# Half-sized products for 55 groups instead of 42, with a plain group between the first two beats of a product run in three places

## The chip, the cores and the metric

The kernel runs on one core of a Trainium2 chip. The metric is the device time of one execution in microseconds, as the median of several runs. TensorE (PE) does the matmuls, VectorE (DVE) and ScalarE (ACT) prepare weights and evict results, GpSimd (POOL) does little here, and SyncE (SP) issues the DMA transfers.

## What is computed

The reference is a stack of transformer blocks on a sequence of 512 tokens with 1024 features. What matters here are its four gated feed-forward layers, in the order ffn1_in0, ffn2_in0, ffn1_in1, ffn2_in1 (an attention and retention mixer stands behind each ffn1, and nothing between ffn2 of layer 0 and ffn1 of layer 1):

```python
D_MODEL, D_FF, SEQ = 1024, 2816, 512
def swiglu(h, w_in, w_out):
    gu = h @ w_in
    a, b = gu[..., :D_FF], gu[..., D_FF:]
    return (jax.nn.silu(a) * b) @ w_out
...
x = x + 0.5 * swiglu(rmsnorm(x, norm_ffn1[l]), w_ffn1_in[l], w_ffn1_out[l])
...
x = x + 0.5 * swiglu(rmsnorm(x, norm_ffn2[l]), w_ffn2_in[l], w_ffn2_out[l])
```

## The kernel before

Everything on the chip is kept transposed: features lie along the 128 partitions and the 512 tokens along the free axis. A product in float32 accuracy is made of three matmuls per tile: weights and activations are split into a high part (fp32r) and a low part, and high times high, low times high and high times low are added up in a PSUM bank.

**Beats.** A planner (`Plan`) writes the whole program as a list of beats. A beat is what PE does with one buffer of 1024 weight columns; there are three such buffers (`w_hi`, `w_lo`, `SPLIT` = 3). Behind each beat the planner hangs a "tail": the work of the other engines, each engine's in the order in which the planner wrote it. The tail of beat i always begins with the split of the weights of beat i + 2: ACT writes `w_hi` (it has to wait until beat i - 1 is done, since it takes that beat's buffer), and DVE writes `w_lo` = raw - w_hi. Each engine works strictly through its own list, so a DVE operation waits for all that stands ahead of it.

**Groups.** A group is two output tiles (256 weight columns over all 1024 features). A plain group takes two beats of 24 matmuls each, 48 matmuls with 512 moving columns, into two banks. `take(2, True)` gives a plain group the free banks with the lowest numbers, of banks 0 to 3 as long as there are any. A product group does the same as seven products of half size in each dimension (Strassen's idea in another arrangement): 84 matmuls with 256 moving columns in four beats: first (two products), second (the forms "difference" and "second"), third (one product, form "third") and fourth (the form "fourth" among its two products). Below they are called A, B, C and D, with the number of the group. They are interleaved from one group to the next: A0 B0 A1 C0 B1 D0 A2 C1 B2 D1 and so on. DVE makes four sums of weight quarters for each group (`st_sum`, line 2813 before), four or five splits of weights (lines 2503 and 2510), three combinations of banks (line 2801), and then scales two tiles at once: `finish_silu` (line 2819, one operation) or, for a hidden group, `finish_hidden` (lines 2825 and 2830, two operations) and `hidden_low` (line 2839, one).

**Forms.** The products need sums of the activations. `make_forms` makes them once per layer: 8 ACT copies (line 2240), four DVE sums "difference", "second", "third" and "fourth" (lines 2849 to 2856), and a split of each on ACT (line 2245) and DVE (line 2860).

**Pieces.** A gated layer has two pieces, 12 and 10 groups, each followed by its part of the output product (`ffn*_out*`). Groups alternate: a silu group (two tiles of `a`), then the hidden group with the two tiles of `b` that belong to it. `by_products` says which groups of a piece are product groups: before, groups 4 to 9 of the first piece and 0 to 7 of the second in the last three layers, and none in ffn1_in0, 42 in all. A plain silu group is evicted by two DVE operations (line 2794); a plain hidden group by two pairs (lines 2655 and 2666) and, in later tails, two `hid_lo` operations (line 2521). In a layer with product groups those evictions are moved one tail back (`apart`).

The lines around a product beat, which set the order within a tail:

```python
        self.into = beat["tail"]
        self.flush()
        self.item("split_hi", i=i + AHEAD)
        self.item("split_lo", i=i + AHEAD)
        ...
        for fn in self.timed.pop(i, ()):
            fn()
        self.run_later()
```

`flush` writes what the beat before has left (copies and combinations), `timed` holds the work of `make_forms`, and `run_later` the evictions that were put off.

Of the kernel before, what the change touches and what calls it, by code (L numbers as in the profile page):

```python
# [7 lines left out]
P = 128  # L8
S = 512
# [38 lines left out]
PLAIN_FIRST = {"ffn1_in0": (12, 10), "ffn2_in0": (4, 0), "ffn1_in1": (4, 0), "ffn2_in1": (4, 0), "mlp_in": (6, 5, 5)}  # L48
# [39 lines left out]
def by_products(name, piece, n_groups):  # L88

    return [PLAIN_FIRST[name][piece] <= i < n_groups - 2 for i in range(n_groups)]  # L90

# [96 lines left out]
class Plan:  # L188
# [59 lines left out]
    def gemm(self, name, n_k, groups, src, evict, first_k=0, n=S, rows=None, tok=None, fresh=True):  # L248


        for tiles in groups:
# [4 lines left out]
            for k0, nk in unit_blocks(n_k, len(tiles)):  # L256
# [7 lines left out]
                beat["load"] = self.load(i, name, at, cols)  # L264
# [136 lines left out]
    def seven_products(self, name, out, finish):  # L401
# [36 lines left out]
        def after_second(units=self.units()):  # L438
            self.copy_out(st, "u2", units, sums[0], 1, LEFT)
        self.waiting.append(after_second)  # L440

        def third():
            self.product_beat([piece(0, second, 0, "t3")], [product("third", 0, sums, False, "u2")])

            def after_third(units=self.units()):
                self.copy_out(st, "u3", units, sums[0], 1, RIGHT)
                self.combine(st, "c22", units, apart[0], 1, RIGHT, "u3", "subtract")
            self.waiting.append(after_third)

        def fourth():  # L450
            first["last"] = second["last"] = self.units()
            self.product_beat([piece(0, first, QUARTER, "t4"), piece(QUARTER, second, QUARTER, None)],
                              [product("right_last", 0, sums, False, "u3"), product("fourth", QUARTER, apart, False, "c22")])

            def after_fourth(units=self.units()):
                self.copy_out(st, "c21", units, sums[0], 0, RIGHT)
                self.bank_over[sums] = ("st_copied", st["c21"])
                self.combine(st, "c12", units, apart[0], 1, LEFT, "u2", "subtract")
                self.bank_over[apart] = ("st_combined", st["c12"])
# [9 lines left out]
    def make_forms(self):  # L469


        start = self.stage_start = self.units()
# [7 lines left out]
        def form(name):  # L480
            it = self.item("form", name=name, values=self.count["form_value"], out=self.add("form"),
# [989 lines left out]
def build(nc, x_in, vec_in, ident_in, tri_in, decay_in, rope_in, sel_in, mem_in, onehot_in, band_in, table_in,  # L1471
# [4 lines left out]
    with ctx:  # L1476
# [140 lines left out]
        def product(it, o):  # L1617

            return bank[it["pair"][o]]
# [1614 lines left out]
```

## Time and profile before

| | |
|---|---|
| median of 3 runs | 3102.11 us (3101.87 to 3102.22) |
| the profiled execution's own time | 3101.85 us |
| its span | 3100.1 us |
| granted TensorE clock, mean | 0.998 |
| PE busy | 3076.7 us, 99% |
| DVE busy | 1782.4 us, 57% |
| ACT busy | 1231.6 us, 40% |
| DMA engines' mean share | 29.2%, 300.78 MB |

A share is an average over the whole span. A matmul's record is longer than the distance between the starts of two matmuls, since they are pipelined: rates are read from a stretch of time and the number of matmuls in it, and idle time of PE only shows where it is longer than that overlap.

### The profile page before, as it was taken

The numbers are of one execution on the slowest core, as the hardware profiler recorded it, in microseconds if no ns is written. First come the engines' busy times: TensorE is split into PE (matmuls) and PEld (weight loads), VectorE is DVE, ScalarE is ACT, GpSimd is POOL, SyncE is SP. The second block draws the span as 40 slices with busy tenths as digits, with TensorE's granted clock in tenths as the row PEclk, the third lists the DMA queues.
The fourth block names the chain that finished last, engine by engine and source line by source line (L and its number), as shares of the span: only waits on it lengthen the run. The fifth ranks groups of instructions, "written<-read, shape, count | busy, mean of one in ns | idle before, by whom it ended". The sixth has DMA issues, their size and how long they took to land.

```text
span 3100.1 us, 40065 instructions
## 1 busy us (share of the span) xinstructions
PE 3076.7 (99%) x15846; PEld 2575.9 (83%) x15846; DVE 1782.4 (57%) x2887; ACT 1231.6 (40%) x1871; POOL 252.9 (8%) x223
## 2 busy tenths in 40 slices
PE   9999999999999999999999999999999999999998
PEld 7888887778889889898877788999888877888887
DVE  6434436555856758495455557758656555563543
ACT  5323335434534445253344335434556433332222
POOL 0000103102000010000031020000300000110001
PEclk9999999999999999999999999999999999999999
DMA  5222322222423232323222232223322233323232
GB/s 157 96 95 93 132 92 72 75 75 95 143 96 109 86 119 86 106 96 130 93 71 75 69 102 102 96 96 109 117 99 87 85 99 99 100 97 100 87 100 78
DMA packets 95930, 303.35 MB, mean 98 GB/s; under 512 B 11184, under 2 KB 21808, under 8 KB 95036
## 3 DMA queue, kind: packets, MB, share of 16 engines
q1 hardware_dynamic: 95744, 300.78, 29.2%
q8 instruction: 127, 2.08, 0.3%
q14 instruction: 59, 0.48, 0.1%
HBM read 298.59 MB, written 5.29 MB: 98 GB/s over the span
## 4 chain that ended last, share of the span: by engine, by line
PE 97%; DVE 1%; issue 0%; DMA 0%; ACT 0%; SPq 0%; POOLq 0%; POOL 0%; DVEq 0%; ACTq 0%
PE bank L2018 77%; PE bank L2047 7%; PE score_ps L2047 4%; PE out_ps L2047 1%; PE score_ps L2018 1%; PE score_ps L1845 1%; PE out_ps L1878 1%; PE turn_ps L1856 1%; PE out_ps L1897 1%; PE score_ps L1887 1%; PE score_ps L1919 1%; PE out_ps L2018 1%; PE score_ps L1969 0%; PE turn_ps L1865 0%; PE turn_ps L1794 0%
## 5 line engine op out<-in xcount | busy, mean ns | idle before, releaser
L2510 DVE TENSOR_TENSOR w_lo<-raw,w_hi 128x1024 fp32r<-128x1024 f32 (+1 forms) x469 | 570.4, 1217 | 861.7 <-ACT w_hi L2080 860.5
L2080 ACT ACTIVATE w_hi<-raw 128x1024 fp32r<-128x1024 f32 (+1 forms) x469 | 479.5, 1024 | 834.1 <-PE bank L2018 763.5
L2018 PE MATMUL bank<-in_hi,w_hi 128*128 128x512 f32 x1960 | 787.8, 402 | 2.0 <-DVE in_lo L2516 1.1
L2018 PE MATMUL bank<-in_hi,w_lo 128*128 128x512 f32 x1960 | 764.9, 390 | 0.0
L2018 PE MATMUL bank<-in_lo,w_hi 128*128 128x512 f32 x1960 | 764.5, 390 | 0.0
L2018 PEld LDWEIGHTS bank<-in_hi,w_hi 128*128 128x128 f32 x1960 | 368.2, 188 | 96.9 <-issue 20.5
L2018 PEld LDWEIGHTS bank<-in_hi,w_lo 128*128 128x128 f32 x1960 | 367.9, 188 | 79.4
L2018 PEld LDWEIGHTS bank<-in_lo,w_hi 128*128 128x128 f32 x1960 | 368.6, 188 | 74.0 <-issue 2.4
L2018 PE MATMUL bank<-hid_hi,w_hi 128*128 128x512 f32 x960 | 374.0, 390 | 0.0
L2018 PE MATMUL bank<-hid_lo,w_hi 128*128 128x512 f32 x960 | 373.5, 389 | 0.0
L2018 PE MATMUL bank<-hid_hi,w_lo 128*128 128x512 f32 x960 | 373.5, 389 | 0.0
L2018 PEld LDWEIGHTS bank<-hid_hi,w_hi 128*128 128x128 f32 x960 | 180.2, 188 | 37.9 <-DVE hid_lo L2839 0.8
L2018 PEld LDWEIGHTS bank<-hid_hi,w_lo 128*128 128x128 f32 x960 | 180.2, 188 | 37.5
L2018 PEld LDWEIGHTS bank<-hid_lo,w_hi 128*128 128x128 f32 x960 | 180.2, 188 | 37.3
L2415 POOL TENSOR_TENSOR ssum<-ssum,tmp 128x512 f32<-128x512 f32 x55 | 77.7, 1412 | 1509.1 <-ACT tmp L2101 1506.2
L2503 DVE TENSOR_TENSOR w_lo<-raw_more,w_hi 128x512 fp32r<-128x512 f32 (+1 forms) x135 | 105.1, 791 | 53.8 <-ACT w_hi L2089 53.5
L2089 ACT ACTIVATE w_hi<-raw_more 128x512 fp32r<-128x512 f32 (+1 forms) x135 | 93.9, 711 | 89.1 <-PE bank L2018 88.1
L2047 PE MATMUL bank<-form_hi_t,w_hi 128*128 128x256 f32 x384 | 109.5, 285 | 5.2 <-DVE w_lo L2503 5.2
L2655 DVE TENSOR_TENSOR tmp<-bank,rstd_b 128x512 f32<-128x512 f32 x153 | 101.2, 683 | 18.1 <-PE bank L2018 15.5
L2047 PE MATMUL bank<-form_lo_t,w_hi 128*128 128x256 f32 x384 | 108.6, 283 | 0.0
L2047 PE MATMUL bank<-form_hi_t,w_lo 128*128 128x256 f32 x384 | 108.6, 283 | 0.0
L2220 ACT ACTIVATE hid_hi<-tmp 128x512 fp32r<-128x512 f32 x78 | 49.0, 632 | 111.8 <-DVE tmp L2666 61.0
(428 smaller groups left out, 4911.9 us busy)
## 6 DMA issues: line engine op xcount, KB each, us to landing
raw<-w_ffn_in SPq DMA_DIRECT2D x121, 512.0 KB, 3.3
raw<-w_mix SPq DMA_DIRECT2D x90, 512.0 KB, 3.3
raw<-w_ffn_out SPq DMA_DIRECT2D x80, 512.0 KB, 3.3
raw<-w_mixb SPq DMA_DIRECT2D x58, 512.0 KB, 3.3
raw_more<-w_ffn_in SPq DMA_DIRECT2D x54, 512.0 KB, 4.6
raw<-w_mlp_in SPq DMA_DIRECT2D x32, 512.0 KB, 3.3
raw<-w_mlp_out SPq DMA_DIRECT2D x28, 512.0 KB, 3.3
raw<-w_w_out SPq DMA_DIRECT2D x16, 512.0 KB, 3.2
```

The costliest lines, as they stand in the source:

```text
L1845: mm = pe.matmul(score[k][:, 0:keys], DST["fq"][hp][64 * k:64 * k + 64, i * P:(i + 1) * P], DST["fk"][hp][64 * k:64 * k + 64, 0:keys], sta ...
L1856: mm = pe.transpose(turn_ps[:, b * P:(b + 1) * P], p[:, b * P:(b + 1) * P], ident[:])
L1878: mm = pe.matmul(out_ps[64 * k:64 * k + 64, i * P:(i + 1) * P], fv[:, b, h * FDH:(h + 1) * FDH], pt[:, b * P:(b + 1) * P], start=b == 0, s ...
L2018: mm = pe.matmul(ps, lhs, rhs, start=first and step == 0, stop=last and step == 2, skip_group_check=True)
L2047: mm = pe.matmul(ps, y, x, start=part["start"] and k == 0 and step == 0, stop=k == TT - 1 and step == 2, skip_group_check=True)
L2080: act.activation(w_hi[:, i % SPLIT, cut], raw_at(ld)[:, cut], ACT.Copy).then_inc(S_["hi_split"], 1)
L2089: hi = act.activation(w_hi[:, i % SPLIT, to], source(part), ACT.Copy)
L2220: act.activation(SRC["hid"][0][part["h"]], tmp[part["t"].b], ACT.Copy).then_inc(S_["hid_hi"], 1)
L2415: pool.tensor_tensor(dst, dst, tmp[s["place"].b][:, 0:n], ALU.add).then_inc(S_["ssum_add"], 1)
L2503: lo = dve.tensor_tensor(w_lo[:, i % SPLIT, to], source(part), w_hi[:, i % SPLIT, to].bitcast(F32), ALU.subtract)
L2510: dve.tensor_tensor(w_lo[:, i % SPLIT, cut], raw_at(ld)[:, cut], w_hi[:, i % SPLIT, cut].bitcast(F32), ALU.subtract).then_inc(S_["lo_split ...
L2655: dve.tensor_tensor(tmp[t.b], product(it, o), RSTD["rstd"], ALU.mult).then_inc(S_["dve_evict"], 1)
```

## The change

Product groups become 55. ffn1_in0 gets groups 8 and 9 of its first piece and 0 to 7 of its second; its forms are made 9 beats later than the layer's start (`FORM_DELAY`), and their first sum waits until six small transfers (`bias_moved`) have left the memory that it overlays. In the first pieces of the other three layers, groups 3 and 5 to 10 are product groups: group 3, a hidden group, is the first product group, and group 4, a plain silu group, stands with its first beat between A and B of group 3 and with its second beat between B and C. Only the last group, a hidden one, stays plain at the end, its two beats between the last groups' C and D. The second pieces of these three layers keep their order. The form "fourth" is made before "third". The plain groups of such a layer may load their weights into the four extra buffers (`raw_more`) too. The values and raw forms lie elsewhere in memory, in two halves.

```diff
-PLAIN_FIRST = {"ffn1_in0": (12, 10), "ffn2_in0": (4, 0), "ffn1_in1": (4, 0), "ffn2_in1": (4, 0), "mlp_in": (6, 5, 5)}
+PLAIN_FIRST = {"ffn1_in0": (8, 0), "ffn2_in0": (3, 0), "ffn1_in1": (3, 0), "ffn2_in1": (3, 0), "mlp_in": (6, 5, 5)}
+FORM_DELAY = {"ffn1_in0": (9, 16 * 6)}
...
 def by_products(name, piece, n_groups):
 
-    return [PLAIN_FIRST[name][piece] <= i < n_groups - 2 for i in range(n_groups)]
+    first = PLAIN_FIRST[name][piece]
+    if piece or name == "ffn1_in0":
+        return [first <= i < n_groups - 2 for i in range(n_groups)]
+    return [first <= i < n_groups - 1 and i != first + 1 for i in range(n_groups)]
...
-        if self.left:
-            self.left.popleft()()
-        self.weight_sums(st, self.beats[-1], "t3", "t4")
-        apart = self.bank_over.take(1)
-        self.product_beat([piece(0, first, 0, "t1"), piece(QUARTER, "t2", 0, "t2")],
-                          [product("difference", 0, apart, True), product("second", QUARTER, sums, False, "m1")])
...
+        def others():
+            self.weight_sums(st, self.beats[-1], "t3", "t4")
+            apart = st["apart"] = self.bank_over.take(1)
+            self.product_beat([piece(0, first, 0, "t1"), piece(QUARTER, "t2", 0, "t2")],
+                              [product("difference", 0, apart, True), product("second", QUARTER, sums, False, "m1")])
...
+        if plain_next and not self.left:
+            self.left.extend([others, third, fourth])
+            return
+        if self.left:
+            self.left.popleft()()
+        others()
         if self.left:
             self.left.popleft()()
         self.left.extend([third, fourth])
...
-                                  lambda: form("second"), lambda: split("difference"), lambda: split("second"),
-                                  lambda: form("third"), lambda: split("third"), lambda: form("fourth"),
+                                  lambda: form("second"), lambda: split("difference"), lambda: form("fourth"),
+                                  lambda: split("second"), lambda: form("third"), lambda: split("third"),
                                   lambda: split("fourth"))):
-            self.after(n + 1, work)
+            self.after(delay + n + 1, work)
```

How the instructions move at the places of which the prediction speaks:

PE at the start of the product run in the first piece of ffn2_in0, before: the first matmul of each part, with the semaphores it waits for (`dve_evict` counts DVE's evictions).

```order
L2018 MATMUL bank_0<-in_hi,w_hi 128x512 [waits lo_split]
L2047 MATMUL bank_2<-in_hi,w_hi 128x256 [waits dve_evict,lo_split]
L2047 MATMUL bank_3<-in_hi,w_hi 128x256 [waits dve_evict]
L2047 MATMUL score_ps<-form_hi_t,w_hi 128x256 [waits form_lo,ret_weighted,lo_split]
L2047 MATMUL bank_2<-form_hi_t,w_hi 128x256 [waits form_lo,st_copied]
```

The same place now.

```order
L2030 MATMUL bank_1<-in_hi,w_hi 128x512 [waits lo_split]
L2059 MATMUL bank_2<-in_hi,w_hi 128x256 [waits dve_evict,lo_split]
L2059 MATMUL bank_0<-in_hi,w_hi 128x256 [waits dve_evict]
L2030 MATMUL bank_1<-in_hi,w_hi 128x512 [waits lo_split,dve_evict]
L2059 MATMUL score_ps<-form_hi_t,w_hi 128x256 [waits form_lo,ret_weighted,lo_split]
L2059 MATMUL bank_2<-form_hi_t,w_hi 128x256 [waits form_lo,st_copied]
```

Between A (banks 2 and 0) and B (`score_ps`) there is now a plain beat into bank 1 (and 3), and the plain group ahead of A had the same pair of banks.

DVE in the tails of the beat A and of the plain beat behind it, first piece of ffn2_in0, now. The first two rows split B's weights; the two `silu_t` rows evict the plain group that stood ahead of A.

```order
L2515 TENSOR_TENSOR w_lo<-raw_more,w_hi 128x512 [waits hi_split]
L2515 TENSOR_TENSOR w_lo<-second_sum,w_hi 128x512
L2874 TENSOR_TENSOR form_lo_t<-form_t,form_hi_t 128x1024 [waits form_hi]
L2533 TENSOR_TENSOR hid_lo<-tmp,hid_hi 128x512 [waits hid_hi] x2
L2806 TENSOR_TENSOR silu_t<-bank_1,rstd_b 128x512 [waits gated,unit_used,rstd]
L2806 TENSOR_TENSOR silu_t<-bank_3,rstd_b 128x512 [waits gated]
L2522 TENSOR_TENSOR w_lo<-raw,w_hi 128x1024 [waits hi_split]
L2825 TENSOR_TENSOR raw<-raw 128x512
```

Before, that eviction stood in the tail two beats ahead of A; A itself took its banks, and a plain beat of another group lay between.

DVE from the tail of A to the split for D at the only new product run in a first piece, ffn1_in0, now (group 8; the `w_lo` rows split the weights of C, then of the next group's B, then of D).

```order
L2867 TENSOR_TENSOR form_t<-form_first 128x1024 [waits form_value,bias_moved]
L2667 TENSOR_TENSOR tmp<-bank_2,rstd_b 128x512 [waits hid_lo,unit_used,rstd]
...
L2813 TENSOR_TENSOR silu_t<-bank_1,silu_t 128x256 [waits st_copied,unit_used]
L2515 TENSOR_TENSOR w_lo<-raw_more,w_hi 128x512 [waits hi_split]
L2874 TENSOR_TENSOR form_lo_t<-form_t,form_hi_t 128x1024 [waits form_hi]
L2515 TENSOR_TENSOR w_lo<-raw_more,w_hi 128x512 [waits hi_split]
L2515 TENSOR_TENSOR w_lo<-second_sum,w_hi 128x512
L2874 TENSOR_TENSOR form_lo_t<-form_t,form_hi_t 128x1024 [waits form_hi]
L2533 TENSOR_TENSOR hid_lo<-tmp,hid_hi 128x512 [waits hid_hi] x2
L2813 TENSOR_TENSOR tmp<-out_ps,tmp 128x256 [waits st_copied,unit_used]
L2515 TENSOR_TENSOR w_lo<-raw,w_hi 128x512 [waits hi_split]
```

The same stretch in ffn2_in0 before: one `form_lo_t` row (that of "fourth") instead of two (those of "third" and "fourth").

```order
L2801 TENSOR_TENSOR silu_t<-bank_3,silu_t 128x256 [waits st_copied,unit_used]
L2503 TENSOR_TENSOR w_lo<-raw_more,w_hi 128x512 [waits hi_split]
L2860 TENSOR_TENSOR form_lo_t<-form_t,form_hi_t 128x1024 [waits form_hi]
L2503 TENSOR_TENSOR w_lo<-raw_more,w_hi 128x512 [waits hi_split]
L2503 TENSOR_TENSOR w_lo<-second_sum,w_hi 128x512
L2521 TENSOR_TENSOR hid_lo<-tmp,hid_hi 128x512 [waits hid_hi] x2
L2801 TENSOR_TENSOR tmp<-out_ps,tmp 128x256 [waits st_copied,unit_used]
L2503 TENSOR_TENSOR w_lo<-raw_more,w_hi 128x512 [waits hi_split]
```

There the sum "third" and its split were done before B; now they stand behind A in ffn1_in0, and B to D follow without a plain beat between.

## Rows read from the trace of the kernel before

**Rows 1.** The page: busy time, share of the span and instructions of each engine.

```profile
PE 3076.7 (99%) x15846; PEld 2575.9 (83%) x15846; DVE 1782.4 (57%) x2887; ACT 1231.6 (40%) x1871; POOL 252.9 (8%) x223
```

**Rows 2.** The page: the chain that ended last, by engine.

```profile
PE 97%; DVE 1%; issue 0%; DMA 0%; ACT 0%; SPq 0%; POOLq 0%; POOL 0%; DVEq 0%; ACTq 0%
```

**Rows 3.** Waits of PE: us in total, times, longest.

```profile
PE bank L2047 <- DVE w_lo L2503: 6.1, 8, 1.1
```

**Rows 4.** Windows: a stretch of plain groups, a second piece's product run.

```profile
208.27:317.07 108.80, 108.80 (x481) 90.12 (x480) 47.23 (x56) 31.99 (x38) 0.00 (x0) 1.00 0.29 94
...
1311.75:1388.18 76.43, 76.43 (x637) 76.38 (x636) 71.38 (x108) 42.56 (x79) 0.00 (x0) 1.00 0.23 79
```

**Rows 5.** Windows: the product runs of the three first pieces.

```profile
809.75:868.92 59.17, 57.01 (x469) 56.38 (x468) 55.95 (x84) 32.95 (x60) 0.00 (x0) 1.00 0.19 65
1161.95:1220.33 58.38, 56.64 (x470) 56.27 (x469) 55.80 (x84) 32.71 (x60) 0.00 (x0) 1.00 0.19 64
1908.16:1967.33 59.17, 57.00 (x469) 56.37 (x468) 55.95 (x84) 32.94 (x60) 0.00 (x0) 1.00 0.19 63
```

**Rows 6.** Timeline of PE: C0, B1 and D0 in the first piece of ffn2_in0.

```profile
819.63 0.36 PE L2047 MATMUL bank<-form_hi_t,w_hi 128*128 128x256 f32 x1 [1.09 <-DVE w_lo L2503]
...
821.95 0.39 PE L2047 MATMUL bank<-form_hi_t,w_hi 128*128 128x256 f32 x1 [0.65 <-DVE w_lo L2503]
...
825.51 0.39 PE L2047 MATMUL bank<-in_hi,w_hi 128*128 128x256 f32 x1 [0.43 <-DVE w_lo L2503]
```

**Rows 7.** Timeline of DVE at the same place.

```profile
818.84 0.68 DVE L2503 TENSOR_TENSOR w_lo<-raw_more,w_hi 128x512 fp32r<-128x512 f32 x1
819.44 1.22 DVE L2860 TENSOR_TENSOR form_lo_t<-form_t,form_hi_t 128x1024 fp32r<-128x1024 f32 x1
820.60 0.69 DVE L2503 TENSOR_TENSOR w_lo<-raw_more,w_hi 128x512 fp32r<-128x512 f32 x1
...
824.16 1.29 DVE L2503 TENSOR_TENSOR w_lo<-raw_more,w_hi 128x512 fp32r<-128x512 f32 x2 [0.64 <-ACT w_hi L2089]
```

**Rows 8.** Timeline of PE: the first matmul of the plain beat ahead of A0.

```profile
804.31 0.39 PE L2018 MATMUL bank<-in_hi,w_hi 128*128 128x512 f32 x1
```

**Rows 9.** Timeline of ACT: split in two halves, a hidden tile, a silu pair.

```profile
804.51 0.63 ACT L2089 ACTIVATE w_hi<-raw_more 128x512 fp32r<-128x512 f32 x1 [4.38 <-PE bank L2018]
805.05 0.61 ACT L2089 ACTIVATE w_hi<-second_sum 128x512 fp32r<-128x512 f32 x1
...
818.63 0.63 ACT L2220 ACTIVATE hid_hi<-tmp 128x512 fp32r<-128x512 f32 x1 [0.70 <-DVE tmp L2666]
...
832.98 1.05 ACT L2231 ACTIVATE silu_t<-silu_t 128x1024 f32<-128x1024 f32 x1
```

**Rows 10.** Timeline of DVE in the two tails ahead of A0.

```profile
803.90 1.29 DVE L2521 TENSOR_TENSOR hid_lo<-tmp,hid_hi 128x512 fp32r<-128x512 f32 x2
805.10 1.28 DVE L2794 TENSOR_TENSOR silu_t<-bank,rstd_b 128x512 f32<-128x512 f32 x2
806.30 0.68 DVE L2503 TENSOR_TENSOR w_lo<-raw_more,w_hi 128x512 fp32r<-128x512 f32 x1
...
807.51 1.21 DVE L2860 TENSOR_TENSOR form_lo_t<-form_t,form_hi_t 128x1024 fp32r<-128x1024 f32 x1
```

**Rows 11.** Timeline of DVE in a product run, ffn2_in0's second piece.

```profile
987.92 0.69 DVE L2503 TENSOR_TENSOR w_lo<-raw,w_hi 128x512 fp32r<-128x512 f32 x1 [0.85 <-ACT w_hi L2089]
...
1000.46 1.22 DVE L2819 TENSOR_TENSOR silu_t<-silu_t,rstd_b 128x1024 f32<-128x1024 f32 x1
...
1009.38 1.22 DVE L2825 TENSOR_TENSOR tmp<-tmp,rstd_b 128x1024 f32<-128x1024 f32 x1
...
1017.44 1.22 DVE L2839 TENSOR_TENSOR hid_lo<-tmp,hid_hi 128x1024 fp32r<-128x1024 f32 x1
...
1020.71 1.22 DVE L2819 TENSOR_TENSOR silu_t<-silu_t,rstd_b 128x1024 f32<-128x1024 f32 x1
```

**Rows 12.** Timeline of DVE: the eviction of a plain hidden pair, first of four.

```profile
815.86 0.68 DVE L2655 TENSOR_TENSOR tmp<-bank,rstd_b 128x512 f32<-128x512 f32 x1
```

More of the change, by code:

```diff
@@ L246, in flush, with gemm @@
             fn()
-    def gemm(self, name, n_k, groups, src, evict, first_k=0, n=S, rows=None, tok=None, fresh=True):
+    def gemm(self, name, n_k, groups, src, evict, first_k=0, n=S, rows=None, tok=None, fresh=True, more=0):
         for tiles in groups:
@@ L263, in gemm @@
                             bank_over=[], others_over=[], half=None, new_k={}, products=None)
-                beat["load"] = self.load(i, name, at, cols)
+                beat["load"] = self.load(i, name, at, cols, more)
                 beat["load"]["last"] = i
@@ L399, in weight_sums, with seven_products @@
             beat["split_end"] += 1
-    def seven_products(self, name, out, finish):
+    def seven_products(self, name, out, finish, plain_next):
         if not self.many_banks:
@@ L452, in fourth @@
             self.product_beat([piece(0, first, QUARTER, "t4"), piece(QUARTER, second, QUARTER, None)],
-                              [product("right_last", 0, sums, False, "u3"), product("fourth", QUARTER, apart, False, "c22")])
+                              [product("right_last", 0, sums, False, "u3"), product("fourth", QUARTER, st["apart"], False, "c22")])
             def after_fourth(units=self.units()):
@@ L467, in form_at, with make_forms @@
         return self.forms.get(form, 0)
-    def make_forms(self):
-        start = self.stage_start = self.units()
+    def make_forms(self, delay, bias):
+        start = self.stage_start = max(self.units(), 1)
         self.forms = {}
@@ L480, in form @@
         def form(name):
-            it = self.item("form", name=name, values=self.count["form_value"], out=self.add("form"),
+            it = self.item("form", name=name, bias=bias, values=self.count["form_value"], out=self.add("form"),
                            source=self.vals.get("form_" + {"second": "difference", "fourth": "second"}.get(name, "")))
@@ L714, in feed_forward @@
                 made = True
-                self.make_forms()
+                self.make_forms(*FORM_DELAY.get(w_in, (0, 0)))
             for i, (tiles, by_seven) in enumerate(zip(groups, seven)):
@@ L724, in evict @@
                             evict_in(outs, units, pair)
-                    self.gemm(w_in, DT, [tiles], self.inp, evict, fresh=tiles is groups[0])
+                    self.gemm(w_in, DT, [tiles], self.inp, evict, fresh=tiles is groups[0],
+                              more=self.stage_start if made else 0)
                     continue
@@ L734, in feed_forward @@
                     awaiting.add(j)
-                    self.seven_products(w_in, out, lambda st, j=j: finish_silu(st, j))
+                    self.seven_products(w_in, out, lambda st, j=j: finish_silu(st, j),
+                                        not (seven + [False])[i + 1])
                 else:
-                    self.seven_products(w_in, out, lambda st, j=j: finish_hidden(st, j))
+                    self.seven_products(w_in, out, lambda st, j=j: finish_hidden(st, j), not (seven + [False])[i + 1])
             assert not self.left
@@ L1626, in product_rows @@
             return bank[it["pair"][o // 2]][:, (o % 2) * 256:(o % 2) * 256 + 256]
-        form_hi, form_lo, form_raw, form_values = m["form_hi_t"], m["form_lo_t"], m["form_t"], m["form_values"]
+        form_hi, form_lo, form_raw = m["form_hi_t"], m["form_lo_t"], m["form_t"]
+        form_values = tiles(m["form_first"]) + tiles(m["form_last"])
         def raw_at(ld):
@@ L2239, in work @@
                     act.wait_ge(S_["unit_used"], it["units"])
-                    act.activation(form_values[:, it["j"], :], xT[it["j"]], ACT.Copy,
+                    act.activation(form_values[it["j"]], xT[it["j"]], ACT.Copy,
                                    scale=gain(dict(it["part"], j=it["j"]))).then_inc(S_["form_value"], 1)
@@ L2843, in work @@
                     dst, before = form_raw[:, f_:f_ + TT, :], form_raw[:, f_ - TT:f_, :]
-                    first, last = form_values[:, 0:TT, :], form_values[:, TT:DT, :]
+                    first, last = m["form_first"], m["form_last"]
+                    if it["bias"]:
+                        dve.wait_ge(S_["bias_moved"], it["bias"])
                     dve.wait_ge(S_["form_value"], it["values"])
```

16 lines of the change are left out of this document (8 added, 8 removed).

## The prediction

> **What bounds the kernel now.** I read the page first: PE is busy for 3076.7 us of a span of 3100.1 [rows 1], and the chain that ended last is 97% PE [rows 2]. So the time is the number of matmuls times their distance, plus the few places where PE waits. The waits of PE come next: in the product stretches it waits for one thing only, DVE's `w_lo`, 8 times and 6.1 us in all [rows 3]. What a matmul costs must be read from windows, since the records overlap. A stretch of 10 plain groups, 480 matmuls, takes 108.80 us, which is 0.2267 us each; a second piece's run of 636 half-width matmuls takes 76.43 us, 0.1202 each [rows 4]. In the same window DVE is busy for 71.38 of 76.43 us: in a product stretch two engines are near their limit, and DVE's 57% on the page hides that. The timeline of DVE shows how near. Its last wait there ends at 987.92; from the `finish_silu` at 1000.46 to the next at 1020.71, two groups later, it takes 20.25 us [rows 11], while PE needs 2 x 84 x 0.1202 = 20.19. DVE can be ahead only by the little that the three weight buffers allow. So I ask of each moved piece of work when DVE does it, not how much it is.
>
> **Fewer matmul columns.** 13 groups change from plain to products: 10 in ffn1_in0, one in each of the three other layers. A plain group is 48 x 0.2267 = 10.88 us, a product group 84 x 0.1202 = 10.10 [rows 4]. That is 0.78 us saved for each, **-10.2 us**. The seven products have 7/8 of the columns, but a matmul of half the width costs 53% of a full one, not 50%, and so the saving is 7%, not 12.5%.
>
> A rule of the Trainium skill would make this larger: "TensorE: Matmul & The Clock Gate", section "Back-to-back issue gap", gives N/2.4 + 2.5 ns for the isolated gap between matmuls at the full clock. By it a product group would be 84 x 109.2 = 9.17 us, a plain one 48 x 215.8 = 10.36, the saving 15.4 us and my sum some 5 us lower. The trace does not agree at either width (120.2 and 226.7 ns), so its rows are used.
>
> **What the old starts cost.** The product runs of the three first pieces are 468 matmuls each, 56.25 us at 0.1202, and take 59.17, 58.38 and 59.17 us [rows 5]. So 2.9 + 2.1 + 2.9 = 7.9 us are lost there. The timeline of PE shows where: C0, B1 and D0 of the first run start late, each behind a `w_lo` [rows 6], and DVE's timeline says why: in these tails it still makes and splits a form and evicts the last plain groups (a `form_lo` lies ahead of B1's weights, 820.60) [rows 7]. In the new order plain beats of 24 x 0.2267 = 5.44 us stand between A and B and between B and C. In each DVE has one weight split of 1.2 us and the forms, so it is done with "third" and "fourth" before C and D come. I take all of it as gone: **-7.9 us** (0 to -7.9).
>
> **A new wait for a bank, three times.** The plain beat behind A takes the very pair of banks that the plain group ahead of A has filled. Their eviction stands in A's own tail, behind the split of B's weights, the split of the form "second" and two `hid_lo`. The trace before has this chain in pieces. ACT starts the two half splits 0.20 us after PE's beat begins and ends them at +1.35 (804.31 to 805.66) [rows 8, 9]. DVE then has two half `w_lo`, 1.21 us from start to start of the next (806.30 to 807.51); the form's split, 1.16 (819.44 to 820.60); two `hid_lo`, 1.20 (803.90 to 805.10); and two `silu_t` evictions, 1.28 [rows 7, 10]. With 0.1 for the hand-over to DVE and 0.1 to PE this is 1.35 + 0.1 + 1.21 + 1.16 + 1.20 + 1.28 + 0.1 = 6.4 us after A's start. A lasts 24 x 0.1202 = 2.88. PE waits for 3.5 us, in each of the three layers: **+10.5 us**. Below: an eviction that had nothing of the form and the `hid_lo` ahead of it would still be 1.2 us late (6.4 - 1.16 - 1.20 - 2.88), so 1.2 each; above 4.5, if ACT or a late `hid_hi` costs another 1.0. I keep 3.5, since every link is a strict order on one engine. Behind the waiting plain beat stand only matmuls; ACT's and DVE's next splits depend on beats already done, so DVE catches up in this time, and the start that follows is the freer.
>
> **Two hidden groups in a row, three times.** The run used to alternate silu and hidden groups. Now group 3 (hidden) is followed by group 5 (hidden). DVE's finish of a hidden group is three operations of 1.22 us, that of a silu group one; taking these 4 x 1.22 = 4.9 from 20.25, a group's common part is 7.7 us [rows 11]. So a hidden group costs DVE 11.3 us against PE's 10.1, a debt of 1.2; a silu group 8.9, which pays it back. Two hidden ones in a row make a debt of 2.4, and what DVE can be ahead is about one debt (before, single ones were carried with no wait on the page). I take 1.2 us in each layer, **+3.6** (0 to 2.4 each).
>
> **The start in ffn1_in0.** Here A, B, A, C, B, D follow each other as in the old starts, so the old loss comes back, 2.9 us [rows 5]. And it is worse by one form: "third" is now summed behind A and split just ahead of C, "fourth" is split behind it, where before only "fourth" stood there. C needs "third" itself; the split ends where `form_lo` ends now, one operation of 1.1 us later than C0's start [rows 6, 7], and D0's weights come later by the same operation. I take 2.9 + 1.1 = **+4.0 us** (2.1 to 5.1). The 8 values and the 4 forms themselves (some 9 us on either engine) lie under plain beats in which DVE is busy for less than half of the time (47.23 of 108.80) [rows 4]; without that cover they would cost 9 us. The wait for `bias_moved` stands some 12 beats in, long after these transfers.
>
> **The end of the first pieces.** Only one plain group is left behind the last silu group's products. Its hidden pair needs that silu: D ends, then come a combination and `finish_silu` in the first output beat, in the second the silu on ACT, which stands behind a weight split that cannot begin before +5.6 (done at 7.7, with 1.05 each), then four evictions of 0.68 on DVE and the last `hid_hi` and `hid_lo` of 0.63 and 0.65 [rows 9, 10, 12]: 7.8 + 2.7 + 0.7 + 0.7 = 11.9. PE wants the last tile at the fourth step of the third output beat, 10.88 + 9 x 0.2267 = 12.9. I cost it at **0**, hidden by two output beats with 1.0 to spare; with one more us of delay it starts to show (0 to 1.0 each).
>
> No transfer is added (a product group loads the same megabyte), and none of SP's or POOL's queue is moved past another; the loads in these pieces are issued sooner.
>
> **Sum.** -10.2 - 7.9 + 10.5 + 3.6 + 4.0 = 0.0. On the profiled execution's own time, 3101.85 us, that is **3101.9 us**; the median of the runs shown is 3102.1, 0.3 above it.
>
> **Rivals.** (1) The new bank wait is not there, because DVE reaches that eviction early. Then the sum is lower by 10.5: 3091. For it speaks only that DVE is idle when A starts; against it the order of the tail, which the plan fixes. (2) DVE never gets ahead in the new runs. Then each of the three hidden groups among the five that finish inside a run costs its full debt of 1.25, 3.75 per layer instead of 1.2: +7.7, 3109.5, which is slower than before. It decides from about 3.3 us per layer. The windows speak for it (55.95 busy of 59.17) [rows 5]; against it that the old runs lost their 2.9 at the start and no more after it, and that the new start leaves DVE two plain beats of rest. (3) The end of the piece shows, by up to 1.0 us in each layer, 3105: a small addition, inside the range. (4) Less is lost in all three disputed places (bank wait 3.0, hidden pair 0, ffn1_in0 2.1): -1.5 - 3.6 - 1.9, 3095.
>
> **How the numbers follow.** A difference of 0.2%, 6.2 us, is about what a measurement here can tell from none; faster is below 3095.9, slower above 3108.3. Forecast, the sum with its small shifts: 0.66. Rival 1: 0.11. Rival 2: 0.11. Rival 4 down to and below 3095.9: 0.08. The old loss partly staying at the new starts, by about 2 us per layer, 3108: 0.04, of which 0.03 slower. Faster 0.19, same 0.67, slower 0.14. The range leaves out rival 1 and the upper half of rival 2: 3095 to 3109.5.
>
> **What would show it.** In the trace after: PE's waits for DVE's `silu_t` eviction, three, of about 3.3 us each (the overlap of records hides 0.16), at the first plain beat behind the first product beat in ffn2_in0, ffn1_in1 and ffn2_in1. No wait for `w_lo` at C0, B1 and D0 there, but one or two of about 1 us some four groups' beats later, at the beats behind the second hidden group's finish. In ffn1_in0's first piece waits of C0 and D0 with 4 us lost in all. The run of its second piece at 0.120 us a matmul. The forecast fails most easily by the bank wait, which is the largest term and was never seen before, and by DVE's debt, which hangs on tenths of a microsecond.

## The result and the profile after

The changed kernel takes 3106.86 us (median of 20 runs, 3103.47 to 3109.16), the kernel before 3102.11 us on the same chips (20 runs, 3101.66 to 3102.57). The ratio is 1.0014, with a 95% interval of 1.0008 to 1.002: slower by 0.14%, some 4.7 us. The forecast was 3101.9 us, no change. The value lies in its range, yet it was off by 5.0 us, and "no change" did not come true: the kernel is slower by more than the measurement is uncertain. The prediction took 0.2%, 6.2 us, for about what can be told from no difference; with 20 runs of each kernel the interval reaches 0.06% to either side. Note also the spread: 5.7 us after, 0.9 us before. The profiled execution took 3108.83 us, near the slow end of that spread.

The page of the changed kernel, busy times and chain; compare [rows 1, 2].

```profile
span 3107.0 us, 41348 instructions
...
PE 3074.3 (99%) x16314; PEld 2595.0 (84%) x16314; DVE 1858.9 (60%) x3009; ACT 1275.8 (41%) x1974; POOL 252.9 (8%) x223
...
PE 96%; DVE 2%; issue 1%; ACT 1%; DMA 0%; SPq 0%; POOL 0%; POOLq 0%; ACTq 0%; DVEq 0%
```

PE is busy for 2.4 us less, and the span is 6.9 us longer: the chain's share of DVE went from 1% to 2%. Where PE waits for DVE now (us in total, times, longest), against [rows 3]:

```profile
PE bank L2030 <- DVE silu_t L2806: 10.7, 4, 3.2
...
PE bank L2059 <- DVE form_lo_t L2874: 2.3, 1, 2.3
...
PE bank L2059 <- DVE tmp L2813: 1.7, 3, 0.6
```

The `w_lo` waits of the old starts are gone from the product runs. In their place stand the three bank waits that were forecast, with a fourth wait for `silu_t` of 1.0 that was not, one for the split of a form, and three for a combination.

The timeline of PE at the first bank wait: the last matmul of A, and the plain beat that takes the banks of the group ahead of A.

```profile
800.39 0.28 PE L2059 MATMUL bank<-in_hi,w_lo 128*128 128x256 f32 x1
803.91 0.79 PE L2030 MATMUL bank<-in_hi,w_hi 128*128 128x512 f32 x1 [3.24 <-DVE silu_t L2806]
804.50 0.63 PE L2030 MATMUL bank<-in_lo,w_hi 128*128 128x512 f32 x1
...
809.62 0.60 PE L2030 MATMUL bank<-in_lo,w_hi 128*128 128x512 f32 x1
810.05 0.41 PE L2030 MATMUL bank<-in_hi,w_lo 128*128 128x512 f32 x1
810.29 0.39 PE L2030 MATMUL bank<-in_hi,w_hi 128*128 128x512 f32 x1
```

From start to start the gap is 803.91 - 800.39 = 3.52 us, 3.40 more than the 0.12 of a matmul (3.5 was forecast). But look at the durations behind it: 0.63 instead of 0.39, and from 804.50 to 809.62 the distance from start to start is twelve times the same, 5.12 us in all, 0.4267 each instead of 0.2267. PE had run at the full clock up to this wait and comes out of it at half of it. The windows of the start (columns: from and to, length, busy time and number of instructions of PE, weight loads, DVE, ACT and POOL, granted clock, DMA share, GB/s) show the clock, first behind each wait in the three layers, then over each whole start, the 96 matmuls from A to the last plain beat:

```profile
803.91:810.05 6.14, 6.14 (x15) 4.79 (x16) 3.75 (x5) 0.61 (x2) 0.00 (x0) 0.50 0.28 88
1159.81:1165.95 6.14, 6.14 (x29) 5.13 (x30) 3.75 (x5) 0.94 (x3) 0.00 (x0) 1.00 0.24 88
1907.69:1913.83 6.14, 6.14 (x20) 4.91 (x21) 3.75 (x5) 0.61 (x2) 0.00 (x0) 0.72 0.25 85
...
797.63:820.70 23.07, 19.83 (x97) 16.89 (x96) 14.29 (x18) 8.63 (x12) 0.00 (x0) 0.85 0.22 59
1153.54:1173.77 20.23, 16.99 (x98) 14.82 (x96) 14.29 (x18) 8.64 (x12) 0.00 (x0) 1.00 0.11 40
1901.42:1923.21 21.79, 18.55 (x98) 15.96 (x96) 14.30 (x18) 8.52 (x12) 0.00 (x0) 0.92 0.11 38
```

0.50 is the lower of TensorE's two levels (1.2 GHz), 1.00 the upper (2.4 GHz), and 0.72 a stretch of both. The three waits have the same length and the same cause, 3.24 us in the records; one is followed by 14 slow matmuls, one by 8, one by none. That is why the three starts take 23.07, 20.23 and 21.79 us. The second, at the full clock, shows what the wait alone costs: 3.55 us more than the same start without a wait (16.68, in e1 below), 0.15 more than its 3.40, since the first distances behind it are a little longer too (0.34 and 0.24 us before they settle at 0.2267). The Trainium skill, "TensorE: Matmul & The Clock Gate", section "Wait — 56ns, not 53.3ns?", gives exactly N ÷ 1.2 GHz from start to start for a cold array, 426.7 ns at 512 columns; the trace agrees, with 0.4267.

The timeline of DVE at the same wait has the chain link by link:

```profile
799.02 0.69 DVE L2515 TENSOR_TENSOR w_lo<-raw_more,w_hi 128x512 fp32r<-128x512 f32 x1 [2.23 <-ACT w_hi L2101]
799.63 0.68 DVE L2515 TENSOR_TENSOR w_lo<-second_sum,w_hi 128x512 fp32r<-128x512 f32 x1
800.23 1.22 DVE L2874 TENSOR_TENSOR form_lo_t<-form_t,form_hi_t 128x1024 fp32r<-128x1024 f32 x1
801.37 1.29 DVE L2533 TENSOR_TENSOR hid_lo<-tmp,hid_hi 128x512 fp32r<-128x512 f32 x2
802.57 1.28 DVE L2806 TENSOR_TENSOR silu_t<-bank,rstd_b 128x512 f32<-128x512 f32 x2
```

A starts at 797.63, `silu_t` ends at 803.85, PE goes on at 803.91: 6.28 us, against 6.4 forecast.

Windows of the product runs (A, C, B, D and so on, without a plain beat between) in the three first pieces, then the first piece's and the second piece's run of ffn1_in0:

```profile
820.70:882.28 61.58, 61.03 (x505) 60.69 (x504) 58.90 (x88) 35.69 (x66) 0.00 (x0) 1.00 0.26 89
1173.77:1235.33 61.56, 61.01 (x505) 60.67 (x504) 58.88 (x88) 35.76 (x66) 0.00 (x0) 1.00 0.26 87
1923.21:1984.78 61.57, 61.02 (x506) 60.68 (x504) 58.89 (x88) 35.68 (x66) 0.00 (x0) 1.00 0.27 86
101.84:121.66 19.82, 17.55 (x134) 17.37 (x133) 17.90 (x26) 10.09 (x17) 0.00 (x0) 0.91 0.08 27
213.08:289.52 76.44, 76.44 (x637) 76.39 (x636) 71.40 (x108) 42.59 (x79) 0.00 (x0) 1.00 0.25 93
```

504 matmuls at 0.1202 are 60.58 us; 1.0 us is lost in each, where 1.2 was forecast. In ffn1_in0's first run 19.82 - 132 x 0.1202 = 3.95 us are lost (4.0 forecast), and there too the clock is not 1.00. Its second run goes at 0.1202.

Where the first of these runs loses its 1.0 us, on PE and on DVE:

```profile
840.12 0.39 PE L2059 MATMUL bank<-form_hi_t,w_hi 128*128 128x256 f32 x1 [0.55 <-DVE tmp L2813]
```

```profile
838.52 1.22 DVE L2851 TENSOR_TENSOR hid_lo<-tmp,hid_hi 128x1024 fp32r<-128x1024 f32 x1
839.65 0.42 DVE L2813 TENSOR_TENSOR tmp<-bank,tmp 128x256 f32<-128x256 f32 x1
...
844.71 1.22 DVE L2837 TENSOR_TENSOR tmp<-tmp,rstd_b 128x1024 f32<-128x1024 f32 x1
```

PE is at the second half of D of group 5, the second hidden group, and waits for the combination at 839.65, which stands behind the `hid_lo` of group 3. From start to start 0.71 us are lost here, the rest in steps of 0.1 behind it. The finish of group 5 begins at 844.71 only.

The books of the profiled execution against that of before, all from starts of matmuls: the stretch from the first plain beat of each piece to the first matmul of its second piece's run, ffn2_in0, 177.92 us before and 181.64 after, +3.72; ffn1_in1 +1.65; ffn2_in1 +2.43; ffn1_in0 with both pieces 344.12 and 341.79, -2.33. That is +5.5 of 6.9. Another 1.1 us lies in the first 28 us of the program, ahead of every change (27.35 before, 28.43 after); this place differs from one execution to the next (26.80 to 27.56 in the traces of the experiments, 27.05 and 27.39 in e5 and e6, which are alike up to there) and is chance.

### The profile page after: what moved, and what is told of

The parts are those of the page before. It is cut to its first block, busy times and chain, and to the rows that moved or that the text cites. A ratio compares the mean times of both kernels' runs of the same rounds, so it can differ in the third digit from the quotient of the medians.

```text
span 3107.0 us, 41348 instructions
## 1 busy us (share of the span) xinstructions
PE 3074.3 (99%) x16314; PEld 2595.0 (84%) x16314; DVE 1858.9 (60%) x3009; ACT 1275.8 (41%) x1974; POOL 252.9 (8%) x223
## 4 chain that ended last, share of the span: by engine, by line
PE 96%; DVE 2%; issue 1%; ACT 1%; DMA 0%; SPq 0%; POOL 0%; POOLq 0%; ACTq 0%; DVEq 0%
PE bank L2030 73%; PE bank L2059 9%; PE score_ps L2059 5%; PE out_ps L2059 2%; PE score_ps L2030 1%; PE score_ps L1857 1%; PE out_ps L1890 1%; PE turn_ps L1868 1%; PE out_ps L1909 1%; PE score_ps L1899 1%; PE score_ps L1931 1%; PE out_ps L2030 0%; PE score_ps L1981 0%; PE turn_ps L1877 0%; ACT w_hi L2101 0%
## 5 line engine op out<-in xcount | busy, mean ns | idle before, releaser
L2522 DVE TENSOR_TENSOR w_lo<-raw,w_hi 128x1024 fp32r<-128x1024 f32 (+2 forms) x414 | 503.3, 1217 | 727.1 <-ACT w_hi L2092 725.8
L2030 PE MATMUL bank<-in_hi,w_hi 128*128 128x512 f32 x1760 | 712.6, 405 | 13.6 <-DVE silu_t L2806 10.7
L2092 ACT ACTIVATE w_hi<-raw 128x1024 fp32r<-128x1024 f32 (+2 forms) x414 | 421.7, 1020 | 731.3 <-PE bank L2030 658.2
L2030 PE MATMUL bank<-in_lo,w_hi 128*128 128x512 f32 x1760 | 688.7, 391 | 0.0
L2030 PE MATMUL bank<-in_hi,w_lo 128*128 128x512 f32 x1760 | 688.6, 391 | 0.0
L2030 PEld LDWEIGHTS bank<-in_hi,w_hi 128*128 128x128 f32 x1760 | 331.7, 188 | 102.0 <-issue 22.2
L2030 PEld LDWEIGHTS bank<-in_hi,w_lo 128*128 128x128 f32 x1760 | 331.4, 188 | 71.9
L2030 PEld LDWEIGHTS bank<-in_lo,w_hi 128*128 128x128 f32 x1760 | 332.2, 189 | 66.3 <-issue 2.4
L2059 PE MATMUL bank<-in_hi,w_hi 128*128 128x256 f32 x388 | 109.8, 283 | 0.0
L2059 PE MATMUL bank<-in_lo,w_hi 128*128 128x256 f32 x388 | 109.8, 283 | 0.0
```

The lines of the kernel that those rows point to most:

```text
L2030: mm = pe.matmul(ps, lhs, rhs, start=first and step == 0, stop=last and step == 2, skip_group_check=True)
L2059: mm = pe.matmul(ps, y, x, start=part["start"] and k == 0 and step == 0, stop=k == TT - 1 and step == 2, skip_group_check=True)
L2092: act.activation(w_hi[:, i % SPLIT, cut], raw_at(ld)[:, cut], ACT.Copy).then_inc(S_["hi_split"], 1)
L2522: dve.tensor_tensor(w_lo[:, i % SPLIT, cut], raw_at(ld)[:, cut], w_hi[:, i % SPLIT, cut].bitcast(F32), ALU.subtract).then_inc(S_["lo_split ...
```

## The experiments

All were timed in five rounds beside the kernel before, whose median was 3102.46 us for the first four and 3102.14 for the last four. My theory from here on: each bank wait costs twice, once as a wait and once as a stretch at the lower clock, and this second cost comes or not by something that the order of the instructions doesn't set. The rivals: the extra time is in the seven groups' longer runs (DVE's debt), or in ffn1_in0.

**e1: other banks for the plain group between A and B.** The group that stands between the first beats takes the next free pair (banks 4 to 6) instead of the lowest.

```diff
-                    banks = self.bank_over.take(2, True)
+                    banks = self.bank_over.take(2, len(self.left) != 3)
```

> The changed kernel, but the plain group that stands inside the first product group takes two of the banks 4 to 6, which nobody has used for long, instead of the pair whose eviction is still to come. The theory (bank wait of 3.24 us in three layers, and after it a stretch at the low clock in some of the layers, by chance) expects that the three waits for the silu_t eviction are gone, that no stretch at a clock of 0.5 is left in the first pieces, that the spread of the times falls from nearly 6 us to under 1.5, and that the median falls by 3 x 3.5 for the waits plus 3 to 4 for the clock, to 3092 to 3094 us. The rival (the spread and the extra 3 to 4 us come from elsewhere, such as the kernel's start, and only the waits go) expects 3096 to 3097 with a spread as wide as before.

Measured: 3092.2 us (3091.38 to 3093.0, 6 runs), ratio 0.9967 [0.9955, 0.9979]; 14.7 us below the changed kernel (15.0 if each is taken against the kernel before in its own rounds). The spread falls from 5.7 to 1.6 us. Windows of the same three starts:

```profile
796.28:812.96 16.68, 16.68 (x97) 14.76 (x96) 14.21 (x18) 8.76 (x12) 0.00 (x0) 1.00 0.33 81
1145.87:1162.55 16.68, 16.68 (x98) 14.76 (x96) 14.21 (x18) 8.76 (x12) 0.00 (x0) 1.00 0.14 49
1890.21:1906.89 16.68, 16.68 (x98) 14.76 (x97) 14.21 (x18) 8.64 (x12) 0.00 (x0) 1.00 0.13 49
```

Exactly the matmuls, 48 x 0.1202 + 48 x 0.2267 = 16.65, at a clock of 1.00. Against the changed kernel's starts this is 6.39 + 3.55 + 5.11 = 15.05 us. Three times the 3.55 of the start at the full clock is 10.65, the waits with the slow first matmuls behind them; the other 4.40 are the lower clock. So the bank wait, which was the whole of +10.5, cost nearly half as much again. The runs themselves are unchanged (61.58 to 61.60), so the rival that puts the loss there falls.

**e2: the eviction earlier in its tail.** The banks stay as in the changed kernel, but in the three tails of A the eviction of the plain silu group stands right behind the split of B's weights, ahead of the form's split and `hid_lo`.

```diff
+        for one, two in zip(self.beats, self.beats[1:]):
+            if one["products"] and one["products"][0]["form"] == "left_first" and not two["products"]:
+                tail = one["tail"]
+                late = [it for it in tail if it["kind"] == "evict_silu"]
+                at = one["split_end"]
+                one["tail"] = tail[:at] + late + [it for it in tail[at:] if it not in late]
```

> The changed kernel with its banks, but in the three tails DVE evicts the plain silu pair right behind the split of B's weights, ahead of the split of the form second and of the two hid_lo. By the strict order on DVE the wait shrinks by 1.16 + 1.20 us, from 3.24 to about 0.9 on the page. If the low clock comes from the length of the gap, it goes: no stretch at 0.5, a spread under 1.5 us, and a median of 3103.5 (the changed kernel's fastest runs) - 3 x 2.35 = 3096 to 3097. If any gap at this place is followed by the low clock, the spread stays as wide and the median is about 3100.

Measured: 3095.93 us, ratio 0.9979 [0.997, 0.9988] (median of ten runs, 3095.53 to 3097.96; an eleventh took 7143.95 us, which nothing in its clock explains and which is left out; with it the median is 3096.18). PE at the first of the three places:

```profile
799.96 0.50 PE L2036 MATMUL bank<-in_hi,w_hi 128*128 128x512 f32 x1 [0.90 <-DVE silu_t L2812]
800.30 0.40 PE L2036 MATMUL bank<-in_lo,w_hi 128*128 128x512 f32 x1
```

Moving two operations of DVE by 2.4 us shortens the wait from 3.24 to 0.90, and the next matmul follows after 0.34 us, as in the start at the full clock (0.59 where the clock is low): no low clock in any of the three. 10.9 us come back, where the shorter waits alone are 3 x 2.34 = 7.0 and the lower clock was 4.4. The spread, 2.4 us, stays above the 1.5 expected; what makes it is not shown. The order of the tail was the cause of the wait, and with a short wait the second cost is gone too in this trace.

**e3: no products in ffn1_in0.** Only the three other layers are changed.

```diff
-PLAIN_FIRST = {"ffn1_in0": (8, 0),
+PLAIN_FIRST = {"ffn1_in0": (12, 10),
```

> The changed kernel with ffn1_in0 all plain, as in the kernel before: 45 product groups. Lost is the saving of 10 x 0.78 = 7.8 us; what comes back is the 4.0 us of waits at its product start, about 1.2 us of the new wait at its fifth beat (which comes from the evictions that are put off one tail), and, if the later first matmul of the changed kernel is its doing and not chance, 1.1 us. So 1.5 to 2.6 us above the changed kernel, 3108.4 to 3109.5. The rival (products in ffn1_in0 are what makes the change slower) expects a time below the changed kernel's.

Measured: 3108.82 us (3106.71 to 3111.46, 11 runs), ratio 1.0022 [1.0013, 1.003]. So ffn1_in0's part is a gain of about 2 us, not the loss; the trace of the changed kernel had 2.33. The waits here are 3.25, 3.24 and 3.25 again, and slow matmuls stand behind the first and the second (some 8 each), none behind the third: another pattern from the same three waits. The granted clocks go with the times: the three runs at 3110.9 us and above have a mean of 0.996, the three at 3107.6 and below 0.998.

**e4: only ffn1_in0 changed.** The other layers keep their four plain groups and the old interleaving; the order of the forms is the new one everywhere.

```diff
-"ffn2_in0": (3, 0), "ffn1_in1": (3, 0), "ffn2_in1": (3, 0)
+"ffn2_in0": (4, 0), "ffn1_in1": (4, 0), "ffn2_in1": (4, 0)
...
-    if piece or name == "ffn1_in0":
-        return [first <= i < n_groups - 2 for i in range(n_groups)]
-    return [first <= i < n_groups - 1 and i != first + 1 for i in range(n_groups)]
+    return [first <= i < n_groups - 2 for i in range(n_groups)]
```

> The kernel before in its last three layers (groups 4 to 9 and 0 to 7), with ffn1_in0's ten product groups and the new order of making the forms: 52 product groups and no plain group inside a product group. Expected: 3102.1 - 7.8 + 4.0 + 1.2 = 3099.5, or 3100.6 if the later first matmul belongs to the change; because fourth is made ahead of third in the old starts too, some 1 us more may be lost in each of the three layers, so up to 3103. A spread under 1.5 us, since no gap is over 2.5. The rival (ffn1_in0 is what costs) expects over 3104.

Measured: 3098.86 us (3097.88 to 3099.57, 11 runs), ratio 0.9988 [0.9979, 0.9997]: -3.6 us. The old start's waits are back:

```profile
PE bank L2057 <- DVE w_lo L2513: 5.6, 7, 1.1
```

The -3.6 are not all ffn1_in0's. The three old product runs take 58.40, 58.42 and 59.09 us here, 0.8 less in all than in [rows 5], though of the change only the order of the forms, their place in memory and the extra buffers of the plain groups reach them. In the trace ffn1_in0 itself is 2.3 us shorter than before (from its first plain beat to the end of the layer's work), as in the changed kernel, and e3 has the same 2.

e1 has the same ffn1_in0. So the three layers without their bank wait are worth 3092.2 - 3098.9 = -6.7. The forecast's terms for those are -2.3 (3 x 0.78) - 7.9 + 3.6 = -6.6. The gain at the starts is real.

**e5: the forms of ffn1_in0 earlier**, on top of e1. They are made 6 beats behind the layer's start, not 9, so that they no longer fall on the products' start.

```diff
-FORM_DELAY = {"ffn1_in0": (9, 16 * 6)}
+FORM_DELAY = {"ffn1_in0": (6, 16 * 6)}
```

> The kernel of e1 (other banks), with the forms of ffn1_in0 begun 6 beats behind the layer's start instead of 9. Third and fourth are then summed and split before the first product beat. If the 4.0 us lost at this start are DVE's work on the forms, most of it goes: only the eviction of the plain hidden pair and its hid_lo are left in those tails, some 0.5 to 1 us, so 3.0 to 3.5 us below e1, 3088.7 to 3089.2. If the loss comes from the products' own weight splits and sums (DVE near its limit anyway), it stays, and the time is that of e1, 3092.2.

Measured: 3089.44 us (3089.26 to 3090.77, 5 runs), ratio 0.996 [0.9948, 0.9973], 2.8 us below e1 (and 3.0 below e7, which was timed in the same rounds and is as fast as e1). What I had not looked at before: behind the wait for `form_lo_t` the clock was low as well. PE there in e1 (timeline), and the window behind it; then both for the same place in e5.

```profile
111.50 0.35 PE L2059 MATMUL bank<-form_hi_t,w_hi 128*128 128x256 f32 x1 [2.26 <-DVE form_lo_t L2874]
```

```profile
111.50:117.50 6.00, 6.00 (x38) 6.00 (x39) 6.00 (x10) 3.34 (x6) 0.00 (x0) 0.72 0.03 3
```

```profile
111.53 0.39 PE L2059 MATMUL bank<-form_hi_t,w_hi 128*128 128x256 f32 x1 [0.66 <-DVE w_lo L2515]
```

```profile
111.53:117.53 6.00, 6.00 (x49) 6.00 (x50) 5.95 (x10) 2.05 (x4) 0.00 (x0) 1.00 0.26 87
```

38 matmuls in 6.00 us against 49: 11 x 0.12 = 1.3 us lost to the clock, besides 2.26 - 0.66 = 1.6 us of wait: 2.9 together, against the 2.8 measured.

**e6: the eviction ahead of the fifth beat**, on top of e5. In a layer with product groups the evictions of plain groups are moved one tail back; ffn1_in0 is such a layer now, and so its first plain silu group is evicted behind the operands of the bias, which the prediction had missed. Here this one eviction stands right behind its tail's weight split.

```diff
+        tail = self.beats[3]["tail"]
+        late = [it for it in tail if it["kind"] == "evict_silu"]
+        at = self.beats[3]["split_end"]
+        self.beats[3]["tail"] = tail[:at] + late + [it for it in tail[at:] if it not in late]
```

> The kernel of e5, and in the tail of the fourth beat of ffn1_in0 DVE evicts the first silu pair before it prepares the bias operands, as in the kernel before the change. The wait of 0.98 us at the fifth beat should go, 1.1 us with the overlap of the records: 1.1 below e5, about 3088. The rival: something else is then just as late there, and nothing is won.

Measured: 3089.22 us (3088.63 to 3090.1, 5 runs), ratio 0.9959 [0.9946, 0.9971], only 0.2 below e5. The last matmul of the fourth beat and the first of the fifth, in e5 and then in e6:

```profile
31.01 0.39 PE L2030 MATMUL bank<-in_hi,w_lo 128*128 128x512 f32 x1
32.41 0.50 PE L2030 MATMUL bank<-in_hi,w_hi 128*128 128x512 f32 x1 [1.01 <-DVE silu_t L2806]
```

```profile
31.37 0.39 PE L2034 MATMUL bank<-in_hi,w_lo 128*128 128x512 f32 x1
31.73 0.50 PE L2034 MATMUL bank<-in_hi,w_hi 128*128 128x512 f32 x1
```

The distance fell from 1.40 to 0.36 us, so the wait is gone. In the profiled execution 0.36 of it was spent by the later start of the program (31.37 against 31.01), ahead of the edit, and the rest, 0.68, stands to the end of the span within some hundredths (3087.5 and 3086.9). Between medians of five runs that overlap in range, the edit's microsecond is not shown; in the trace it is.

**e7: `hid_lo` later**, on top of e1. The new wait of 0.55 in the run is for a combination that stands behind `hidden_low` of the first product group, group 3. Here `hidden_low` moves to the end of the next tail.

```diff
...
+                tail, then = self.beats[i + 9]["tail"], self.beats[i + 10]["tail"]
+                low = [it for it in tail if it["kind"] == "hidden_low"]
+                tail.remove(low[0])
+                then.append(low[0])
```

> The kernel of e1, and the hid_lo of the first product group in the three first pieces (one DVE operation of 1.22 us) moved behind the combination and the weight split that follow it. The theory that two hidden groups in a row leave DVE in debt when the fourth product wants its combined bank expects that the three waits for the combination (0.55 us each on the page, 1.0 us of the run's time) shrink or go: up to 3.0 us, 3089.2 to 3091. A debt that is only put off appears some beats later, and the time is then that of e1, 3092.2.

Measured: 3092.39 us (3091.52 to 3092.55, 6 runs), ratio 0.9968 [0.9956, 0.998], the same as e1. PE's waits in this kernel:

```profile
PE score_ps L2066 <- DVE w_lo L2522: 1.7, 3, 0.6
```

The three waits for the combination are gone, and three of the same length for weights have come, at the start of the next group's D (at 841.20 in the first of the three layers, 8.7 us further on in the run than the wait in e1). The runs take 61.61, 61.62 and 61.59. It is a debt of DVE's time, and not the order of one tail: what is moved is only waited for elsewhere.

**e8: a longer bank wait.** The changed kernel, with the sum of the form "third" moved from the next tail to a place ahead of the late eviction: no work more, but the wait grows by one operation.

```diff
...
+                third = [it for it in two["tail"] if it["kind"] == "form"]
+                two["tail"] = [it for it in two["tail"] if it["kind"] != "form"]
+                at = [it["kind"] for it in one["tail"]].index("evict_silu")
+                one["tail"][at:at] = third
```

> The changed kernel with its banks, and DVE sums the form third ahead of the eviction instead of one tail later: no work more, but the three waits grow by 1.14 us, from 3.24 to about 4.4. Of the waits alone the fastest runs would be 3103.5 + 3.4 = 3106.9. If the length of the gap brings the low clock on, it comes in more of the three layers or at each, by 2 to 3 us each time: a median of 3110 to 3115, more than the 3103.5 + 3.4 + 3.4 = 3110.3 that the same chance as in the changed kernel gives. If the chance does not depend on the length, 3110.

Measured: 3112.01 us (3111.99 to 3112.53, 5 runs), ratio 1.0032 [1.002, 1.0045]; 5.15 above the changed kernel. The last of the three waits in PE's timeline, and windows behind each:

```profile
1910.39 0.80 PE L2036 MATMUL bank<-in_hi,w_hi 128*128 128x512 f32 x1 [4.38 <-DVE silu_t L2812]
```

```profile
802.76:808.76 6.00, 6.00 (x19) 4.88 (x20) 2.62 (x4) 0.61 (x2) 0.00 (x0) 0.72 0.31 90
...
1158.58:1164.58 6.00, 6.00 (x14) 4.75 (x15) 2.62 (x4) 0.61 (x2) 0.00 (x0) 0.50 0.27 90
...
1910.39:1916.39 6.00, 6.00 (x16) 4.81 (x17) 2.62 (x4) 0.61 (x2) 0.00 (x0) 0.57 0.25 87
```

At the full clock 26 matmuls fit into 6.00 us. Here it is 19, 14 and 16: some 7 + 12 + 10 = 29 are missing, 29 x 0.2267 = 6.6 us. The waits themselves grew by 3 x 1.14 = 3.4; with the 6.6 - 4.4 that the clock takes more than in the changed kernel's trace that is 5.6, against 5.15 between the medians. The spread of the runs fell from 5.7 to 0.5 us. With the longer wait the lower clock comes in all three layers of the traced execution; that it does so in the others too, and that chance has less part in the time, fits the small spread but is not shown.

## Why the forecast was off, by its own steps

**Fewer matmul columns, -10.2:** right. The second pieces' runs stand at 0.1202 us a matmul, the rate on which it rests.

**What the old starts cost, -7.9:** right. The start without the bank wait takes 16.68 us for 16.65 us of matmuls in e1, and e4, which has the old starts (7.2 us lost in its trace, with the new order of the forms), is 6.7 us longer than e1.

**A new wait for a bank, three times, +10.5:** this is the step that failed. Its mechanism, its place and its length were right (3.40 against 3.5, and the chain of DVE's operations as listed), and it was priced as a wait alone. In the profiled execution the three waits cost 10.65 us and the low clock behind them 4.40, 15.05 in all. For the median: e1 lies 14.7 us below the changed kernel, so the clock takes 14.7 - 10.65 = 4.0 there (4.4 with the 15.0). That is most of the miss of 5.0; the fifth beat below, +1.2, is the rest, and the smaller differences of the other terms nearly cancel. The fast end of the changed kernel's runs, 3103.5, is where the sum would be with the fifth beat's 1.2 added and no lower clock behind these waits (3103.1); which of those runs had none is not shown, since only one execution has a trace.

**Two hidden groups in a row, +3.6:** 3 x 1.0 = 3.0, and e7 shows that it is a debt of DVE's time, as forecast. The place and the reason were not right. PE was to wait for weights behind the second hidden group's finish; it waits for a combination at 840.12, 4.6 us before that finish begins (844.71). Only one hidden group has been finished by then, so the second can't have made this debt, and that the size came out near is in part luck. It is e7, with the operation put off, in which PE waits for weights and behind that finish. Which part of DVE's list at the new start makes the debt was not tested.

**The start in ffn1_in0, +4.0:** the size was right by luck. 3.95 us were lost, but some 2.4 as the wait of C for the split of the form "third" and 1.4 as low clock; D had no wait. In e5, with the forms elsewhere, 2.8 us of it come back.

**The end of the first pieces, 0:** right; the output products run without a wait (288 matmuls in 65.31 us; at 0.2267 each they are 65.29).

**Missed:** the fifth beat of ffn1_in0, +1.2, a consequence of `apart` that now holds for a fourth layer. The prediction asked what was queued at the places it named and not which other tails the same switch reorders.

Of the rivals, the first (no bank wait) is refuted by the trace, and what it would have been worth is e1. The second (DVE never gets ahead) is refuted by the 61.58 us of the runs, the third (the end of the piece shows) by the 65.31, the fourth (less is lost at all three places) by the 3.40, 1.0 and 3.95 us. None of them had a stall that costs more than its length.

e6 is the fastest version: 3089.2 us, 0.41% below the kernel before. The whole difference to the changed kernel, 17.6 us, is one choice of banks, one number of beats and one place in a tail.

## What to carry to other kernels

Price a new stall on a saturated PE with what follows it: behind a wait of 3.24 us in the records this kernel lost another 1.5 us on average to the lower clock in each of three places, and behind one of 0.90 us none. Before putting other work between two beats, ask which banks it takes and whose eviction stands where in the strict queue; taking another pair, or moving one eviction ahead of two operations that are needed only later, was worth 14.7 and 10.9 us here. And when a kernel's spread widens from 0.9 to 5.7 us with the same work, look for stretches of lower granted clock in its trace: a mean clock that goes from 0.998 to 0.996 is already some 6 us of 3100 (an estimate, 0.002 x 3100).

## What the hardware showed that was not expected

Behind a gap of PE the clock may fall to the lower level although PE was busy without a break before and is again after. Counted over the traces of this case, in the product stretches: behind 3.24 or 3.25 us (the changed kernel, e3) in 4 of 6 cases; behind 4.38 us (e8) in 3 of 3; behind 2.26 or 2.27 us (`form_lo_t` in ffn1_in0) in 4 of 6, among them the changed kernel, e1, e4 and e7 but not e2 and e8; behind 0.90 us (e2) in none of 3, nor behind the waits of up to 1.1 us of the kernel before. Outside these stretches every trace has one wait of 1.67 us for `rgw` (2247.99 before), and the clock stays up behind it in all ten. The low stretches lasted from about 3 to 6 us, and some began with the first matmul behind the gap, others 0.3 to 1.5 us later (1907.69 and 1909.20 in the changed kernel). What decides in a given case is not shown: the same instruction sequence gave 14, 8 and 0 slow matmuls behind three equal waits.
